# Output weights split during the projection and kept in DRAM, in place of a split by GpSimd during attention

## The reference

```
h  = rmsnorm(x, g_norm_mix);  proj = h @ w_in              # q, k, v of two groups of heads
oa = neighbourhood_attention(qa, ka, va, rpb)              # 8 heads on a 32 x 64 grid of tokens
ob = windowed_gqa_sink(rope(qb), rope(kb), vb, sink)       # 8 query heads, 2 key heads, window 128
o  = concat(rmsnorm(oa, g_out_na), rmsnorm(ob, g_out_swa))
x  = x + o @ w_out                                         # the gains can be put into the rows of w_out
x  = x + (silu(h2 @ w_gate) * (h2 @ w_up)) @ w_down,  h2 = rmsnorm(x, g_norm_ffn)
return rmsnorm(x, g_final)
```

## Time and profile before

| | |
|---|---|
| median of 3 runs | 2259.54 us (2259.07 to 2263.42) |
| the profiled execution | 2259.97 us, span 2258.2 us |
| TensorE busy | 2208.8 us, 98% of the span |
| VectorE, ScalarE, GpSimd busy | 1440.5, 922.3, 327.8 us |
| queries and keys of the neighbourhood heads | 120 to 300 us |
| attention, window rounds | 614 to 766 us |

### The profile page before, as it was taken

How to read it: one execution, slowest core, us unless ns; L and a number is a source line. 1 busy time by engine, 2 the same in 40 slices (tenths; PEclk the granted TensorE clock), 3 DMA queues, 4 the chain that set the end, 5 groups by cost and what they waited for, 6 DMA issues and landing times.

```text
span 2258.2 us, 33189 instructions
## 1 busy us (share of the span) xinstructions
PE 2208.8 (98%) x11464; PEld 1818.5 (81%) x11464; DVE 1440.5 (64%) x2747; ACT 922.3 (41%) x1824; POOL 327.8 (15%) x304
## 2 busy tenths in 40 slices
PE   7999999999999999999999999999999999999998
PEld 6888888788877788778888887888888877888886
DVE  4412143399899777776666657665656578565776
ACT  4411121288888633343333334433333333131342
POOL 3370001145334100011212120000000002020100
PEclk9999999999999999999999999999999999999999
DMA  6472425789954275675545457323232286353544
GB/s 225 140 186 99 140 87 148 201 217 246 235 143 111 83 226 200 224 265 175 189 165 199 154 209 263 128 80 131 80 131 73 102 305 234 104 177 108 191 145 152
DMA packets 274677, 376.68 MB, mean 167 GB/s; under 512 B 15258, under 2 KB 182306, under 8 KB 269168
## 3 DMA queue, kind: packets, MB, share of 16 engines
q1 hardware_dynamic: 266528, 354.15, 49.3%
q0 software_dynamic: 5568, 11.87, 2.0%
q10 hardware_dynamic: 2448, 8.91, 1.4%
HBM read 237.77 MB, written 140.31 MB: 167 GB/s over the span
## 4 chain that ended last, share of the span: by engine, by line
PE 89%; DVE 6%; DMA 2%; issue 2%; ACT 1%; POOL 0%; DVEq 0%; ACTq 0%; SPq 0%
PE late_psum L2047 11%; PE late_psum L2048 11%; PE late_psum L2049 11%; PE late_psum L2078 6%; PE late_psum L2080 5%; PE late_psum L2079 5%; PE late_psum L1017 4%; PE late_psum L997 4%; PE late_psum L527 3%; PE late_psum L528 3%; PE late_psum L529 3%; PE late_psum L555 3%; PE late_psum L554 3%; PE late_psum L556 3%; PE late_psum L985 2%; PE late_psum L1396 2%
## 5 line engine op out<-in xcount | busy, mean ns | idle before, releaser
L2047 PE MATMUL late_psum<-ff_h,ff_ring 128*128 128x512 f32 x1232 | 479.9, 390 | 5.9 <-DVE ff_acts L1907 3.0
L2049 PE MATMUL late_psum<-ff_h,ff_ring 128*128 128x512 f32 x1232 | 479.3, 389 | 0.0
L2048 PE MATMUL late_psum<-ff_h,ff_ring 128*128 128x512 f32 x1232 | 479.3, 389 | 0.0
L2047 PEld LDWEIGHTS late_psum<-ff_h,ff_ring 128*128 128x128 f32 x1232 | 231.2, 188 | 55.9 <-DVE ff_h L1868 3.9
L2049 PEld LDWEIGHTS late_psum<-ff_h,ff_ring 128*128 128x128 f32 x1232 | 231.2, 188 | 48.1
L2048 PEld LDWEIGHTS late_psum<-ff_h,ff_ring 128*128 128x128 f32 x1232 | 231.2, 188 | 47.7
L2078 PE MATMUL late_psum<-ff_d,ff_a 128*128 128x512 f32 x616 | 240.6, 391 | 8.3 <-DVE ff_x L1967 5.3
L2079 PE MATMUL late_psum<-ff_d,ff_a 128*128 128x512 f32 x616 | 239.7, 389 | 0.0
L2080 PE MATMUL late_psum<-ff_d,ff_a 128*128 128x512 f32 x616 | 239.7, 389 | 0.0
L1967 DVE TENSOR_TENSOR ff_x<-late_psum,ff_x 128x512 f32<-128x512 f32 x224 | 153.6, 689 | 121.4 <-PE late_psum L2080 121.0
L1863 DVE TENSOR_TENSOR ff_ring<-ff_raw,ff_ring 128x512 fp32r<-128x512 f32 x176 | 127.5, 726 | 104.3 <-ACT ff_ring L1740 104.1
(11 more groups left out here) (159 smaller groups left out, 4148.9 us busy)
## 6 DMA issues: line engine op xcount, KB each, us to landing
acts_scratch<-ff_acts SPq DMA_DIRECT2D x22, 1792.0 KB, 7.8
ff_a<-acts_scratch SPq DMA_DIRECT2D x24, 960.0 KB, 5.1
ff_raw<-in_w_gate SPq DMA_DIRECT2D x44, 512.0 KB, 3.8
ff_raw<-in_w_up SPq DMA_DIRECT2D x44, 512.0 KB, 3.9
ff_d<-down_scratch SPq DMA_DIRECT2D x21, 768.0 KB, 6.3
att_q_stack<-qk_scratch SPq DMA_DIRECT2D x56, 256.0 KB, 5.2
ffn_in_scratch<-mix_h_stage SPq DMA_DIRECT2D x8, 1792.0 KB, 6.2
ff_h<-ffn_in_scratch SPq DMA_DIRECT2D x14, 1024.0 KB, 7.6
```

The source lines that it names most:

```text
L2047: pe.matmul(out_bank, whi[:, k], hhi[:, :, k], start=(k == 0 and not onto), stop=False, skip_group_check=onto)
L2048: pe.matmul(out_bank, whi[:, k], hlo[:, :, k], start=False, stop=False, skip_group_check=onto)
L2049: last = pe.matmul(out_bank, wlo[:, k], hhi[:, :, k], start=False, stop=(k == 3), skip_group_check=onto)
```

## The change

The output weights are scaled and split in the projection. At even steps j below 16 SyncE loads 128 raw rows of `w_out` (512 KB) into `out_raw`; at odd steps ScalarE multiplies them by their gains into the high part, VectorE makes the low part, and SyncE stores both (1 MB) into a scratch tensor in DRAM. There is one `out_raw` and one `out_parts` buffer: the next load waits for VectorE, the next multiplication for the store. They lie over the buffers of the normed input, its gains and one input tile, which are done with by then, and under `w4`, so the split of slice 12 (step 20) now waits for the last of these stores. GpSimd loads the gains after its first two weight splits. In attention GpSimd's 24 operations, their loads and the load of the gains are gone; instead it issues 8 loads of 1 MB, one every 12 units from round 4 on, the first when the neighbourhood heads' last value products are done. `weights_split` waits for these loads. The order of TensorE's instructions is the same.

```diff
@@ -207,6 +211,39 @@
 
     def near_arrived(eng):
         eng.wait_ge(near_in, 16 * len(near_parts))
+
+    def out_weights_stored(eng):
+        eng.wait_ge(out_stored, 16 * KT)
+
+    def load_out_weights(k):
+
+        if k == 0:
+            sp.wait_ge(turned, NT)
+        else:
+            sp.wait_ge(out_lo_done, k)
+        if k < 4:
+            sp.dma_start(out_raw[:], w_out[k * P:(k + 1) * P, :]).then_inc(out_in, 32)
+            return
+        for e in range(2):
+            r0 = AW + (k - 4 + 4 * e) * HD
+            sp.dma_start(out_raw[e * HD:(e + 1) * HD, :], w_out[r0:r0 + HD, :]).then_inc(out_in, 16)
+
+    def store_out_weights(k):
+        sp.wait_ge(out_lo_done, k + 1)
+        sp.dma_start(out_dram[k], out_parts[:].bitcast(F32)).then_inc(out_stored, 16)
+
+    def out_weights_hi(k):
+        if k == 0:
+            act.wait_ge(gains_in, 48)
+        act.wait_ge(out_in, 32 * (k + 1))
+        if k >= 1:
+            act.wait_ge(out_stored, 16 * k)
+        nc.scalar.mul(out_parts[:, 0], out_raw[:], gains[:, k:k + 1]).then_inc(out_hi_done, 1)
+
+    def out_weights_lo(k):
+        dve.wait_ge(out_hi_done, k + 1)
+        nc.vector.scalar_tensor_tensor(out=out_parts[:, 1], in0=out_raw[:], scalar=gains[:, k:k + 1],
+                                       in1=out_parts[:, 0], op0=ALU.mult, op1=ALU.subtract).then_inc(out_lo_done, 1)
 
     def load_w(n):
         earlier = [i for i in range(n) if slot_of[i] == slot_of[n]]
...
@@ -259,6 +296,8 @@
                 src = stage[:, j % 2, :].bitcast(F32)
                 sp.dma_start(qk_dram[part, r0:r0 + P, cols], src) \
                     .then_inc(stored[j % 2], 16)
+            if j < 2 * KT:
+                (store_out_weights if j % 2 else load_out_weights)(j // 2)
             if j == 3:
                 for n in range(8, 12):
                     load_w(n)
@@ -299,6 +338,12 @@
             pool.wait_ge(w_hi_by_pool, i + 1)
             nc.gpsimd.tensor_tensor(w_part(1, n), raw_of(n), w_part(0, n), ALU.subtract) \
                 .then_inc(w_lo_by_pool, 1)
+        with nc.allow_non_contiguous_dma(reason="gains, one for each partition"):
+            pool.dma_start(gains[:, 0:4], g_na.rearrange("a (k p) -> p (a k)", p=P)).then_inc(gains_in, 16)
+            for e in range(2):
+                pool.dma_start(gains[e * HD:(e + 1) * HD, 4:8],
+                               g_swa[:, e * 4 * HD:(e + 1) * 4 * HD].rearrange("a (k p) -> p (a k)", p=HD)) \
+                    .then_inc(gains_in, 16)
         for t in range(NT):
             pool.wait_ge(tok_done, t + 1)
             store_v(pool, t, 1, v_stored_by_pool)
...
@@ -385,6 +430,8 @@
                 act.wait_ge(stored[j % 2], 32 * (j // 2))
 
             nc.scalar.mul(staged(out_hi, j), result(j), 1.0 if j < 16 else -SCALE).then_inc(res_hi, 1)
+            if j < 2 * KT and j % 2:
+                out_weights_hi(j // 2)
             for n in split_at(V_STEPS + j):
                 split_hi(n)
         for t in range(NT, 3 * NT):
@@ -473,6 +520,8 @@
                 low = nc.vector.scalar_tensor_tensor(out=staged(out_lo, j), in0=result(j), scalar=-SCALE,
                                                      in1=staged(out_hi, j), op0=ALU.mult, op1=ALU.subtract)
             low.then_inc(res_lo, 1)
+            if j < 2 * KT and j % 2:
+                out_weights_lo(j // 2)
             for n in split_at(V_STEPS + j):
                 split_lo(n)
         dve.wait_ge(rope_in, 32)
...
@@ -833,48 +881,19 @@
                     last = nc.gpsimd.tensor_tensor(out, m, b, ALU.subtract)
             last.then_inc(bias_made, 1)
 
-    def load_w(k):
-        if k < 4:
-            pool.dma_start(w_raw[:, k % 2, :], w_out[k * P:(k + 1) * P, :]).then_inc(w_in[k % 2], 32)
-            return
-        for e in range(2):
-            r0 = AW + (k - 4 + 4 * e) * HD
-            pool.dma_start(w_raw[e * HD:(e + 1) * HD, k % 2, :], w_out[r0:r0 + HD, :]) \
-                .then_inc(w_in[k % 2], 16)
-
     def gpsimd(proj):
         make_bias(0, proj)
         with pool.Fori(1, NEAR_ROUNDS) as r:
             make_bias(r)
 
 
-        with nc.allow_non_contiguous_dma(reason="gains, one for each partition"):
-            pool.dma_start(gcol[:, 0:4], g_na.rearrange("a (k p) -> p (a k)", p=P)).then_inc(gains_in, 16)
-            for e in range(2):
-                pool.dma_start(gcol[e * HD:(e + 1) * HD, 4:8],
-                               g_swa[:, e * 4 * HD:(e + 1) * 4 * HD].rearrange("a (k p) -> p (a k)", p=HD)) \
-                    .then_inc(gains_in, 16)
-        load_w(0)
-        load_w(1)
-        pool.wait_ge(gains_in, 48)
-        def wait_units(step):
-
-            pool.wait_ge(shifted, UNITS * (NEAR_ROUNDS + 1) + 5 * step)
-
+        proj.out_weights_stored(pool)
         for k in range(KT):
-            raw, w_hi, w_lo = w_raw[:, k % 2, :], w_pool[:, k, :], w_pool[:, KT + k, :]
-            pool.wait_ge(w_in[k % 2], 32 * (k // 2 + 1))
-            wait_units(3 * k)
-            nc.gpsimd.tensor_scalar(raw, raw, gcol[:, k:k + 1], None, ALU.mult).then_inc(w_scaled, 1)
-            pool.wait_ge(w_scaled, k + 1)
-            wait_units(3 * k + 1)
-            nc.gpsimd.tensor_copy(w_hi, raw).then_inc(w_hi_done, 1)
-            pool.wait_ge(w_hi_done, k + 1)
-            wait_units(3 * k + 2)
-            nc.gpsimd.tensor_tensor(w_lo, raw, w_hi, ALU.subtract).then_inc(w_lo_done, 1)
-            if k + 2 < KT:
-                pool.wait_ge(w_lo_done, k + 1)
-                load_w(k + 2)
+
+            pool.wait_ge(shifted, UNITS * (NEAR_ROUNDS + 1) + 12 * k)
+            if k == 0:
+                pool.wait_ge(pv_done, NEAR_PT_BUFS // 2 + NT * NEAR_ROUNDS)
+            pool.dma_start(f32(w_pool[:, k::KT, :]), out_dram[k]).then_inc(out_weights_in, 16)
 
     def exp(kind, r, u):
         i, t = u % SN_BUFS, u // 2
@@ -1064,8 +1083,6 @@
         self.att_stats = [self.at(f"att_{n}", 176128 + 32 * i, [P, 8]) for i, n in enumerate(("negmax", "total", "rtotal"))]
         self.win_mask = self.at("att_win_mask", 176256, [P, 3 * P])
         self.sinks = self.at("att_sinks", 177792, [P, SWH])
-        self.gcol = self.at("att_g_out", 177824, [P, KT])
-        self.w_raw = self.at("att_w_out_raw", 177856, [P, 2, D])
 
         self.p_raw = self.at("w_raw", 0, [P, 4, 1024])
         self.p_xn = self.at("x_normed", 16384, [P, D])
@@ -1079,6 +1096,9 @@
             ("rope_c", 63488, [P, SWH, ROPE]), ("rope_s", 64000, [P, SWH, ROPE]))]
         self.p_stats = [self.at(f"{n}1", 64512 + 64 * i, [P, NT]) for i, n in enumerate(("ssq", "msq", "inv", "rstd"))]
         self.p_ident = self.at("ident1", 64768, [P, P])
+        self.p_gains = self.at("g_out", 65280, [P, KT])
+        self.p_out_raw = self.at("w_out_raw", 16384, [P, D])
+        self.p_out_parts = self.at("w_out_parts", 20480, [P, 2, D], F32R)
         self.p_hT = self.at("hT", 65376, [P, NT, 2, KT, P], F32R)
         self.p_tok = self.at("x_tile", 196448, [P, 2, D])
         self.p_out_hi = self.at("stage_hi", 204640, [P, 2, BANK], F32R)
```

25 lines of the change are left out of this document (15 added, 10 removed).

## The result

The changed kernel takes 2264.64 us (median of 20 runs, 2259.66 to 2269.49) against 2260.45 us of before (20 runs, 2258.18 to 2263.56): a ratio of 1.0018, 95% interval [1.0011, 1.0024]. It is 0.18% slower: the interval excludes 1, but the difference is under the 0.2% from which on the prediction speaks of a change. The time lies outside the range of the prediction. The profiled execution has a span of 2262.6 us, 4.4 more than before.

What follows compares the result with a forecast made beforehand. TensorE, busy 98% of the span, was taken as the bound. Attention saves 4.8 us and all else costs 0: 2259.97 - 4.8 = 2255.2 us profiled, median 2254.7; range 2253.4 to 2260.0 us.

Steps and rivals of the forecast that it cites:

- The gain in attention: Window rounds 4 to 7: removing GpSimd's 24 operations saves TensorE 4.8 us, bounds 4.1 to 6.1.
- Rival C: Attention: the waits go but TensorE gains only 0 to 2 us, time 2257.5 to 2259.5; chance 0.08.
- The loads in attention at no cost: Attention: GpSimd's 8 loads of 1 MB, one every 12 units, make nothing wait; cost 0.
- The loop of 9.7 us a block: Projection: one output-weight block's loop takes 9.7 us of an 11.2 us budget, making good 1.5 us a pair of steps.
- TensorE doesn't wait: Projection: late output-weight blocks stay within the allowed lateness, so TensorE has no gap; cost 0.
- The lateness of block 2: Projection: block 2 of the output weights starts 11 to 13 us late, behind four weight loads and the table.
- The allowance of 12.6 us at block 6: Projection: block 6 may be 12.6 us late before slice 9's cast behind it delays step 17; 7 to 9 expected.
- The 18.8 of the banks: Projection: a block may be 18.8 us late before TensorE's step 2k+6 waits for staged step 2k+2.
- Rival A: Projection: SyncE's queue is slower beside the table, TensorE stalls 2 to 8 us, time 2256.7 to 2262.7; chance 0.20.
- Rival B: Projection: slow queue, longer table and nothing made good; late casts cost 10 us, time 2265, slower than before; chance 0.08.
- The 175 GB/s: Projection: a rival's rate for SyncE's queue beside the table, putting block 2 20 to 22 us late.

Runs made afterwards that it cites:

- load_first: The changed kernel with each load of output weights issued ahead of its step's staged pair, still one raw buffer: 2256.42 us, 0.9981 of the kernel before.
- projection_half: The changed kernel with its projection part kept, but GpSimd's 24 operations back in attention: 2270.99 us, 1.0037 of the kernel before.

## Why the prediction was wrong

- **The gain in attention, 4.8 us (4.1 to 6.1): right.** Rounds 4 to 7 measure 4.9 us less in every version with the loads, and the round of 36.44 us, made up of each position's least distance, came out at 36.45. Rival C falls.
- **The loads in attention at no cost: right.** They landed in 6.0 us, TensorE was 40.00 us busy of 40.
- **The loop of 9.7 us a block: the step that failed.** It counted one staged pair a loop, "a store of 1.05 MB, a staged pair of 0.52 and a load of 0.52: 2.1 MB". In each 11.2 us of steps there are two. A loop that is on time has the second one in its idle part; a late one has both beside store and load. The term is 2.62 MB and 11.0 us (11.2 by the prediction's rate), and the 1.5 us a block that were to be made good are nearly nil: block 7, said to be about on time, is still some 16 late. load_first, in which no pair stands ahead of the load, gives the 9.7. The step that follows from it, "TensorE doesn't wait", "Cost 0", measures 7.0 us.
- **The lateness of block 2, 11 to 13 us: too small by 4 to 5.** Measured 16.6. The gap needs both misses: 12 us late and nothing made good stays under the 12.6 allowed at block 6, and 16.6 with 1.5 made good on each of the last three or four blocks would be 12.1 or 10.6 there. The same miscount is in it: between block 1's remainder and block 2's multiplication, 149.3 to 171.1 us, the queue carries store, four loads, two pairs and a load, 4.7 MB, and after 1.5 us of latency that is 232 GB/s, not 252. The four loads and the table are not two terms to be added: without the table block 2 is 6.7 late, without the four loads ahead 6.9, so taking away either takes off some 10 us of 16.6. That the bytes of the one pass slowly beside the other fits this; it is argued, not shown.
- **The allowance of 12.6 us at block 6: right.** 16.7 late gives a gap of 4.1 by it; 4.3 was measured. The 18.8 of the banks was not contradicted: 16.6 late at block 2, 17.2 at block 3, and no wait at steps 6 to 12.
- **The price of a gap: a term that was missing.** Rivals A and B priced a stall by its length. After this one TensorE ran twelve products at the lower clock, 2.5 us more on top of 4.5.
- **Rival A: not its way.** The 175 GB/s did not come, it was 232, and block 2 was not 20 to 22 us late. The 4.5 us of stall lie in its range of 2 to 8, but at step 17 and for a cast.
- **Rival B had the place and nearly the sum.** Its condition, a loop of 11.1 us in which nothing is made good, is what happened, though by more bytes and not by a slower rate; its "step 17 about 3" was 4.3. Its other 7 us, at steps 10 or 12, did not come. It got 0.08, and should have had more: the forecast rested on a loop 1.5 us under its budget, and one more pair, 1.46 us, uses that up.

What stays open: by the terms the changed kernel should be 2.1 us slower than before (7.0 less 4.9). It measures 4.2 and 4.6, intervals from 2.5 to 5.4 and from 1.4 to 6.6: the first leaves 2.1 out, the second does not. projection_half too is slower by 9.0 where its trace shows 6.7 in the stage, but that lies in its interval, and its profiled execution (2267.55 us) was the fastest of the five. The versions without a gap lie 3.4 to 5.8 us under before, where 4.9 are due. So the kernels with the gap may lose some 2 us more in the common execution than in the profiled one. Two traces of the same kernel show that the slow products behind the gap last 5.3 us in one and 3.1 in the other, 1 us of cost apart. Against it stands that the first of them, with the longer stretch, took 2264.57 us, the median, and has its other 2 us in the near rounds and behind attention. No run here settles it.

## What to carry to other kernels

When a queue feeds a loop of load, compute and store in an order that is fixed by hand, count the bytes for the late case as well: what the engine has put off in waiting comes out in a burst, right beside the transfer that it waits for. A loop whose reserve is no longer than one such transfer keeps the lateness that it once has, and the cost comes where something urgent stands behind it; put the urgent instruction, or the load, ahead, and the lateness costs next to nothing. Price a gap of TensorE by its length and by what the clock does behind it.
